# Ends of the attentions of layers 1 and 2 of a fused three-layer kernel: the first seven slices of an output tile are made while the last head pair is gated, and queries are rounded in two steps

## What is computed

```python
# layer 1 (A): windowed attention, 16 heads on 4 key heads, a sink per head, context keys for all
q, k, v, g = split(h @ w_in);  q, k = rope(q), rope(k)
p = softmax(concat(q k_loc^T * scale + mask, q k_ctx^T * scale, sink))
y = ((p @ v) * silu(g)) @ w_o            # for the 512 tokens and for the 256 context tokens
x = x + gate * y;  ctx = ctx + gate_c * yc
# layer 2 (B): latent attention, 16 heads, all 768 keys
y = ((softmax((qn kn^T + qr kr^T) * scale) @ v) * silu(g)) @ w_o;  x = x + gate * y
x = rmsnorm(x, final_g)
# layer 3 (C and D): neighbourhood attention with bias (8 heads) beside an mLSTM (4 heads), one output projection
```

## Time and profile before

| | |
|---|---|
| median of 3 runs | 1179.33 us (1176.61 to 1180.14) |
| the profiled execution's own time | 1179.01 us |
| its span | 1177.2 us |
| PE (TensorE matmul) busy | 1106.4 us, 94% of the span |
| DVE (VectorE), ACT (ScalarE), POOL (GpSimd) busy | 61%, 55%, 35% |
| attention of layer 1, layer 2, layer 3, about | 103 to 400 us, 571 to 763 us, 885 to 974 us |
| PE at half the granted clock, seen in windows of 1 us | from about 328, 366, 403, 765, 1103, 1110 us, and behind the last matmul |

### The profile page before, as it was taken

One profiled execution on the slowest core, in us unless ns is written; L12 is line 12 of the kernel. 1 busy time (PEld: TensorE's weight loads), 2 busy tenths in 40 slices (PEclk: granted clock), 3 DMA queues, 4 the chain that ended last, 5 costly groups with the idle time before them and its releaser, 6 DMA issues.

```text
span 1177.2 us, 20182 instructions
## 1 busy us (share of the span) xinstructions
PE 1106.4 (94%) x7408; PEld 903.1 (77%) x7408; DVE 721.3 (61%) x1582; ACT 651.9 (55%) x1363; POOL 416.7 (35%) x512
## 2 busy tenths in 40 slices
PE   4899999999998799999899999999999999999896
PEld 0588778877886689877677878798878778887685
DVE  6365666676668526263877878645767774526545
ACT  4614455555556526642766768746567653447633
POOL 1633112202120334674300002316654326446871
PEclk9999999999999999999999999999999999999898
DMA  9741333422112221132222121042212405213112
GB/s 354 266 144 59 138 141 139 149 108 99 46 28 90 74 72 37 54 123 75 57 88 66 29 82 46 7 157 81 77 48 74 148 19 144 73 54 126 38 35 72
DMA packets 34253, 109.33 MB, mean 93 GB/s; under 512 B 4516, under 2 KB 7076, under 8 KB 33772
## 3 DMA queue, kind: packets, MB, share of 16 engines
q1 hardware_dynamic: 34156, 108.05, 27.6%
HBM read 101.39 MB, written 2.11 MB: 88 GB/s over the span
## 4 chain that ended last, share of the span: by engine, by line
PE 76%; DVE 9%; ACT 4%; POOL 4%; issue 3%; DMA 2%; SPq 1%; DVEq 0%; POOLq 0%; ACTq 0%
PE PS L673 32%; PE PS L656 14%; PE PS L789 8%; PE PS L777 7%; PE PS L968 6%; PE PS L1032 3%; DMA AF<-wstream 2%; POOL AR L2509 2%; PE PS L873 1%; PE PS L708 1%; ACT AF L1255 1%; DVE AF L1956 1%; DVE AF L2035 1%; DVE AD L2331 1%; PE PS L1007 1%
## 5 line engine op out<-in xcount | busy, mean ns | idle before, releaser
L2509 POOL TENSOR_TENSOR AR<-AF,AR 128x256 fp32r<-128x256 f32 x396 | 300.0, 790 | 605.8 <-ACT AR L1132 605.7
L673 PE MATMUL PS<-AR 128*128 128x512 f32 (+1 forms) x2208 | 454.9, 363 | 11.9 <-POOL AR L2509 4.1
L673 PEld LDWEIGHTS PS<-AR 128*128 128x128 f32 x2208 | 367.6, 191 | 79.3 <-issue 18.5
L656 PE MATMUL PS<-AR 128*128 128x256 f32 (+4 forms) x1284 | 245.9, 328 | 7.9 <-ACT AF L1255 3.3
L656 PEld LDWEIGHTS PS<-AR 128*128 128x128 f32 (+1 forms) x1284 | 181.1, 191 | 43.0 <-issue 22.0
L1264 ACT ACTIVATE AF<-PS 128x512 f32<-128x512 f32 (+3 forms) x192 | 124.3, 648 | 109.6 <-PE PS L777 105.5
L1255 ACT ACTIVATE AF<-PS,AF 128x512 f32<-128x512 f32 (+3 forms) x192 | 140.7, 733 | 22.2 <-DVE AF L2308 13.2
L777 PE MATMUL PS<-AF 128*128 128x128 f32 x864 | 128.1, 275 | 10.0 <-DVE AF L1956 6.7
L777 PEld LDWEIGHTS PS<-AF 128*128 128x128 f32 x864 | 100.2, 140 | 34.9 <-issue 15.2
L1132 ACT ACTIVATE AR<-AF 128x1024 fp32r<-128x1024 f32 x99 | 103.4, 1052 | 42.1 <-PE PS L968 27.9
L789 PE MATMUL PS<-AF 128*64 128x128 f32 x1728 | 115.7, 279 | 2.1 <-DVE AF L1963 2.1
(11 more groups left out here) (212 smaller groups left out, 1129.6 us busy)
## 6 DMA issues: line engine op xcount, KB each, us to landing
AF<-wstream SPq DMA_DIRECT2D x171, 512.0 KB, 4.6
AF<-x_in SPq DMA_DIRECT2D x2, 1024.0 KB, 8.6
AD<-rows SPq DMA_DIRECT2D x4, 512.0 KB, 5.8
out<-AF SPq DMA_DIRECT2D x16, 128.0 KB, 1.9
AF<-AF SPq DMA_DIRECT2D x28, 64.0 KB, 2.0
AF<-rpb_band SPq DMA_DIRECT2D x8, 224.0 KB, 4.6
BIAS<-rpb_band SPq DMA_DIRECT2D x8, 224.0 KB, 4.7
AF<-ctx_in SPq DMA_DIRECT2D x1, 1024.0 KB, 5.3
```

Of the source, the lines that this page charges most:

```text
L656: mm = pe.matmul(out, stationary, moving, start=i == 0, stop=i == len(products) - 1)
L673: mm = pe.matmul(out[:, 0:t1 - t0], a, b, start=k == 0 and i == 0, stop=k == nk - 1 and i == 2)
L2509: ins = pool.tensor_tensor(w[:, 1, at:at + 256], raw(c)[:, at:at + 256], w[:, 0, at:at + 256].bitcast(F32), ALU.subtract)
```

## The change

Three things are written otherwise.

1. Layer 1, end: `attend` no longer ends with the wait for `o_read`. Slices 0 to 6 of the tile A.o0.0 (21 matmuls of 256 columns) stand ahead of slice 7 of A.o0.1, slice 7 of A.o0.0 behind it, and then the wait for `o_read`.
2. Layer 2, end: the same wait moves behind B.o0.0. ScalarE rounds part 1 of pairs 0 and 1 in its last but one step, of pairs 2 to 6 behind its last step and of pair 7 when that is gated, and then part 0. VectorE makes the rests of pairs 0 to 6 behind its last normalise and ahead of the last gate_output. In every attention the values of step m1-2 (in layer 3 of m1-3) stand ahead of the second turn when m == m1.
3. Layer 1, queries: `split_q(p)` is called twice, for half 0 at m % 6 == 3 and for half 1 at m % 6 == 4. Each call is one rounding and one subtraction.

```diff
--- before.py
+++ after.py
@@ -809,14 +809,15 @@
                     if m0 <= m - behind < m1:
                         banks_read(m - behind == m0, 4, 5, 6)
                         turn(2 * (m - behind))
-                    if values_first and m0 <= m - behind - 1 < m1:
+                    ahead = values_first or m == m1
+                    if ahead and m0 <= m - behind - 1 < m1:
                         weigh_values(m - behind - 1)
                     if m < m1:
                         banks_read(m == m0, 2, 3)
                         scores(2 * m + 1)
                     if m0 <= m - behind < m1:
                         turn(2 * (m - behind) + 1)
-                    if not values_first and m0 <= m - behind - 1 < m1:
+                    if not ahead and m0 <= m - behind - 1 < m1:
                         weigh_values(m - behind - 1)
                     if m < m1 or values_first:
                         for name in fillers(m):
@@ -880,9 +881,11 @@
                 if p == 0:
                     pe.wait_ge(kz_done, 2)
 
-            attend(0, A_END, ready_a, lambda m: fillers_a(m // 6 + 1, m % 6), values_first=True)
+            attend(0, A_END, ready_a, lambda m: fillers_a(m // 6 + 1, m % 6), values_first=True, drained=False)
+            project("A.o0.0", "A.o0", OA, 0, H, k1=KD - 1)
             make("A.o0.1:78")
-            project("A.o0.0", "A.o0", OA, 0, H)
+            project("A.o0.0", "A.o0", OA, 0, H, k0=KD - 1)
+            pe.wait_ge(o_read, group_of[A_END - 1] + 1)
             for j in range(1, KD):
                 project(f"A.o{j}.1", f"A.o{j}", OA, H, T)
             for j in range(1, KD):
@@ -940,11 +943,13 @@
                     pe.wait_ge(kr_in[p], 16 * (p + 1))
 
             attend(A_END, B_END, ready_b,
-                   lambda m: fillers_b((m - A_END) // 4 + 1, (m - A_END) % 4) if (m - A_END) // 4 + 1 < N_PAIR else [])
+                   lambda m: fillers_b((m - A_END) // 4 + 1, (m - A_END) % 4) if (m - A_END) // 4 + 1 < N_PAIR else [],
+                   drained=False)
             for j in range(KD):
                 project(f"B.o{j}.1", f"B.o{j}", OB, H, S, ready=out_ready(8) if j == 0 else None)
                 if j == 0:
                     project("B.o0.0", "B.o0", OB, 0, H, ready=out_ready(16))
+                    pe.wait_ge(o_read, group_of[B_END - 1] + 1)
             for j in range(1, KD):
                 project(f"B.o{j}.0", f"B.o{j}", OB, 0, H)
                 if j == 1:
@@ -1438,11 +1443,23 @@
                 if 24 <= m - A_END < 31:
                     need("B.o0", m - A_END - 23)
 
-            attend(A_END, B_END, evacs_b)
-            act.wait_ge(o_read, 16 + 8)
-            for part in (1, 0):
-                for j in range(KD):
-                    out_high("B", j, OB, [(OG[:, :, PART[part]], part * H, part * H + H)])
+            def out_high_b(j, part):
+                act.wait_ge(o_read, 16 + j + 1)
+                out_high("B", j, OB, [(OG[:, :, PART[part]], part * H, part * H + H)])
+
+            def feeds_b(m):
+                if m == B_END - 2:
+                    act.wait_ge(s_ready, 2 * B_END)
+                    for j in range(2):
+                        out_high_b(j, 1)
+                if m == B_END - 1:
+                    for j in range(2, KD - 1):
+                        out_high_b(j, 1)
+
+            attend(A_END, B_END, evacs_b, feeds_b)
+            out_high_b(KD - 1, 1)
+            for j in range(KD):
+                out_high_b(j, 0)
 
             def squares_2(part, j):
 
@@ -1913,16 +1930,14 @@
                 dve.wait_ge(cos_done, r + 1)
                 signal(dve.tensor_tensor(QP[:, 0:S], QP[:, 0:S], COSP, ALU.add), rope_sum, r + 1)
 
-            def split_q(p):
+            def split_q(p, half):
                 dve.wait_ge(tanh_done, 2 * p + 1)
                 if p >= 2:
                     dve.wait_ge(s_ready, pair_scored("A", p - 2))
-                for half, h in enumerate(ROWS_OF):
-                    ins = dve.tensor_copy(QA[h, p % 2, half, :], QP[h, :])
-                step(ins)
-                for half, h in enumerate(ROWS_OF):
-                    dve.tensor_tensor(QA[ROWS_OF[1 - half], p % 2, half, :], QP[h, :],
-                                      QA[h, p % 2, half, :].bitcast(F32), ALU.subtract).then_inc(q_lo, 1)
+                h = ROWS_OF[half]
+                step(dve.tensor_copy(QA[h, p % 2, half, :], QP[h, :]))
+                dve.tensor_tensor(QA[ROWS_OF[1 - half], p % 2, half, :], QP[h, :],
+                                  QA[h, p % 2, half, :].bitcast(F32), ALU.subtract).then_inc(q_lo, 1)
 
             def gate(name, dst, count, at=0):
 
@@ -1941,7 +1956,8 @@
                 for t in range(3 * j, 3 * j + 3):
                     read(dve.tensor_copy(VA[:, t, :], wait_acc(f"A.v.{t}")[:, 0:256]), f"A.v.{t}")
             rope_q(0)
-            split_q(0)
+            split_q(0, 0)
+            split_q(0, 1)
             gate("A.qg0.c", OGC[:, 0, :], 1, C)
             gate("A.g0.x", OG[:, 0, :], 2)
 
@@ -2023,8 +2039,8 @@
                         out_low_a(j)
                 elif s == 2:
                     rope_q(p)
-                elif s == 3:
-                    split_q(p)
+                elif s >= 3 and s < 5:
+                    split_q(p, s - 3)
 
             attend(0, A_END, others_a, later_a)
             out_low_a(7)
@@ -2146,15 +2162,22 @@
                     for name in fillers_b(p, s):
                         ada_part(name) if name.startswith("ada") else low_b(name)
 
-            attend(A_END, B_END, others_b)
-
+            def out_low_b(j, part):
+
+                dve.wait_ge(og_hi, 8 + (1 - part) * KD + j + 1)
+                dve.tensor_tensor(OB[1][:, j, PART[part]], OG[:, j, PART[part]], OB[0][:, j, PART[part]].bitcast(F32),
+                                  ALU.subtract).then_inc(og_lo, 1)
+
+            def later_b(m):
+                if m == B_END - 1:
+                    for j in range(KD - 1):
+                        out_low_b(j, 1)
+
+            attend(A_END, B_END, others_b, later_b)
+            out_low_b(KD - 1, 1)
             step(dve.tensor_tensor(GAINF, GAIN[:, 2, :, 0], col("fg", 0, KD), ALU.mult))
-            for part in (1, 0):
-                for j in range(KD):
-                    n = 8 + (1 - part) * KD + j + 1
-                    dve.wait_ge(og_hi, n)
-                    dve.tensor_tensor(OB[1][:, j, PART[part]], OG[:, j, PART[part]], OB[0][:, j, PART[part]].bitcast(F32),
-                                      ALU.subtract).then_inc(og_lo, 1)
+            for j in range(KD):
+                out_low_b(j, 0)
 
             def update_2(part, j):
 
```

## The result

The changed kernel takes **1205.5 us** (median of 4 runs, 1203.1 to 1206.1) where the kernel before takes 1178.3 us (4 runs, 1176.6 to 1180.1): ratio 1.023, 95% interval 1.021 to 1.025. It is slower, as forecast, but by 27 us and not by 13; 1205.5 lies outside the range. The profiled execution took 1205.9 us, its span is 1204.1 us, and the mean granted clock fell from 0.989 to 0.973.

What follows compares the result with a forecast made beforehand. TensorE was taken as the bound (76% of the chain, no other engine above 9%), so its stands and lower clock cost time. Stall 15.5, ends -4.0 and -3.4, falls +4.8 make +12.9 on 1179.0: 1192 us, range 1184 to 1198.

Steps and rivals of the forecast that it cites:

- "1.55 us" for a half: Layer 1's queries: rounding 0.56 us, subtraction 0.97 and about 0.02 between make one half 1.55 us on VectorE.
- "Three at 1.6 us": New clock falls at layer 1's pair starts: one at pair 5, two among pairs 1 to 4; +4.8 us.
- 2.3 us at pairs 1 to 4, 3.1 and 1.6 us after, 15.5 in sum: Layer 1's pair starts: TensorE delayed by the second half, 9.2 + 3.1 (pair 5) + 3.2 (pairs 6, 7) = 15.5 us.
- "The change does help first": Before pairs 6 and 7 one half frees VectorE at 323.28, not 324.82; still 1.6 us later each, 3.2 for two.
- The ends: Ends of layer 1's and layer 2's attention: matmuls fill TensorE's gaps, clock falls vanish; -4.0 and -3.4 us.
- The weight load: Pair starts: load waits with its matmul, by the row; the skill's rule would save some 0.2 us each, 1.4 in all.
- The rest: Layer 3's reorder costs nothing; VectorE's step between the halves of the very first rounding adds under 0.1 us.
- a hidden half: Layer 1's pairs have unseen slack that hides the second half, so only the ends count: 1171.6 us, chance 0.06.
- one half given back: Layer 1's pairs: half of the 15.5 us stall is given back, no new fall comes: 1179 us, chance 0.07.
- ends without effect: Attention ends bring nothing, as the clock falls anyway and weights or gate hold TensorE: 1199 us, chance 0.08.

Runs made afterwards that it cites:

- experiment 3: Changed kernel plus spare TensorE matmuls ahead of the wait for the queries' second half: twenty, 1196.4 us; second kernel, 13 (pairs 1 to 4) or 19 (5 to 7), 1193.0 us.
- experiment 5: Changed kernel with the next gate weights split one attention step later and 9 (pairs 1 to 4) or 15 (5 to 7) spare matmuls: 1185.3 us.
- experiment 4: Changed kernel with ScalarE and GpSimd splitting the next gate weights one attention step later: 1193.3 us, ratio 1.014 to the kernel before.
- experiment 7: Changed kernel with queries rounded in one piece (ends alone), plus seven spare matmuls ahead of the scores of pairs 6 and 7: 1170.4 us.
- Experiment 6: Changed kernel with queries rounded in two steps for pairs 6 and 7 only, in one piece for pairs 1 to 5: 1178.2 us.
- experiment 1: Changed kernel with both query halves rounded in one step again, so only the two ends are changed: 1172.2 us, ratio 0.9945 to the kernel before.

## Why the prediction was right in its sign and wrong in its size

- **"1.55 us" for a half.** This step failed for pairs 1 to 6. The rows behind it, two roundings in 1.12 and two subtractions in 1.94 us, were taken at another place in the program. The change moved the half to where GpSimd had split the gate's weights all along, beside VectorE work that was not slowed (the maximum took 0.76 us there and without GpSimd). There a rounding takes 0.97 us for 0.56 and a subtraction 1.36 for 0.95, 0.8 us a half, 4.8 us for six, which the prediction had at nothing. Experiments 3 and 5 agree: 41.33 against 40.56 us from pair 1 to pair 2. Pair 7, with no GpSimd, has the old price. That it is GpSimd is shown by the overlap and its absence at six pairs and one, and by moving it; experiment 4 moved ScalarE's part of the splitting with it, but that had ended at 139.07 when the half began at 139.35.
- **"Three at 1.6 us"** (new falls of the clock). This step failed most: +4.8 us was forecast, at most +8.0. There were five new ones and not three, and their length was mis-sized: 6.83 us, where every fall in the trace of before ahead of the last matmul had 3.41. A long one costs 3.0 us at pairs 1 to 3, the short one at pair 4 cost 1.5, close to the 1.6 of the prediction. The two old falls, held to cost nothing new, became long ones as well. By the traces the seven falls cost 16.5 us, 14.7 more than the two of before (1.8 us, experiment 7); by the medians 12.5. What the prediction read of the clock, falls behind stands of 1.67 us and more and not behind shorter ones, left out two stands before the attention in the same trace, of 2.36 us (to 25.86) and 2.03 us (to 48.66), that had none; what makes a fall come, and what makes it long, no run here shows.
- **2.3 us at pairs 1 to 4, 3.1 and 1.6 us after, 15.5 in sum.** Right as a reckoning of VectorE's place: 2.27 us in experiment 4. The sum is read from experiment 5 against experiment 7, since neither has a fall in the attention: 14.9 us between the medians, 15.8 in the traces, of which 9.4 to pair 4's scores (forecast 9.2) and 6.4 behind them (forecast 6.3). In the changed kernel itself the stall was 3.1 us at pairs 1 to 4. (Where the prediction says that VectorE's place is read from rows 2, the rows are the earlier trace rows.)
- **"The change does help first"** at pairs 6 and 7. Experiment 6 has 5.9 us for both against 3.2; the stand of 4.92 us at pair 6 holds 0.8 us of GpSimd's. The rest would fit the longer fall at pair 7, but no run separates it.
- **The ends.** -4.0 and -3.4 us forecast, -4.0 and -3.3 measured, no fall at either; experiment 1 gives -5.9 for both by the medians and -7.4 in its trace.
- **The weight load.** The changed kernel's scores had waited 3.08 us and then began with the load and the matmul together at 141.76. The row was the better guide than the rule of the Trainium skill that the prediction sets beside it.
- **The rest.** Layer 3 and all behind layer 2's end gave 0.0 us, as said. The rivals of a hidden half, of one half given back and of ends without effect are all out.

The attention's sum, forecast and in the traces: 15.5 and 15.8 us for the stall, 0 and 4.8 for GpSimd, 4.8 and 14.7 for the falls, 20.3 and 35.3 together over the ends alone. The sign was right for the reason given, and the error of 15 us is two thirds falls and one third GpSimd.

Both could have been asked of the profile beforehand. POOL has a row at pair 4's start of the kernel before, four subtractions from 253.81 for 2.84 us, and the half was to begin at 253.99. And the same trace has the price: for pair 0 the first of the two subtractions ran beside GpSimd and took 1.38 us for 0.97.

```profile
97.48 2.21 POOL L2509 TENSOR_TENSOR AR<-AF,AR 128x256 fp32r<-128x256 f32 x2 [7.42 <-ACT AR L1132]
97.72 1.38 DVE L1924 TENSOR_TENSOR AR<-AF,AR 64x768 fp32r<-64x768 f32 x1
```

The Trainium skill says what such a neighbour means. "SBUF — State Buffer", section "SBUF: two separate sides", says that GpSimd and those VectorE instructions that use a second SBUF port share one pair of ports, that it is locked for a whole instruction, and that the later engine waits. The trace agrees that both lose: VectorE's two instructions 0.41 us each, and GpSimd's four took 3.85 us for the 2.84 that they took beside the maximum. That an instruction waits for another's whole length it doesn't show: one after the other, all six would need 1.51 + 2.84 = 4.35 us, and they were done 3.85 us after the first began (spans on GpSimd are rough).

## What to carry to other kernels

Price an instruction at the place where it will stand, with what the other engines do there, and ask of GpSimd first when VectorE reads and writes SBUF. Where work is moved behind the last thing that an engine does before another one needs it, the whole of it is a wait, and what TensorE then loses at the lower clock can be as large again: here 16 us of foreseen stall came with nearly 20 us of GpSimd and clock. Another place for the work took most of it away: with the second half between the two maxima the halves cost 6 us and not 33. Try the parts of a change apart: its two ends alone gain 6 us, and the third part hid that.

## What the runs showed of the hardware

- The granted clock at 0.50 came in stretches of 3.41 us and of 6.83 us. At stands of 3.08 us and more in the changed kernel six of seven were 6.83 us; at stands of 2.27 us in experiment 4 there were none three times and one of 3.41 us. The stand alone doesn't fix it: with the queries alone, a stand of 3.08 us had no fall at pair 1 and one of 3.41 us at pair 2.
- What a fall cost differed by its place: for one of 6.83 us 3.0 us at pairs 1 to 3, and 1.6 to 2.2 at pairs 5 to 7, where it began in the stand; for one of 3.41 us 1.5 us at pair 4, and in experiment 7 1.6 at pair 6 and 0.2 at pair 7.
- Spare matmuls in a wait removed each fall that they were put ahead of; in one trace a fall came at another place, behind the attention (experiment 3's second kernel, 418.1). Each of these 128x128 float32 matmuls has two records (140 were issued in the attention, 280 are recorded), 0.22 us together (20 of them in 4.4 us).
- GpSimd's subtractions and VectorE's rounding and subtraction of the queries slow each other: 0.97 and 1.36 us for 0.56 and 0.95 on VectorE, 3.85 for 2.84 us on GpSimd. VectorE's maximum, which reads PSUM, kept its 0.76 us beside GpSimd.
